# The second layer's experts as fp32 matmuls on two 64-column halves, with 22 weight tiles fetched ahead

## What is computed

```python
def _expert_choice_ffn(h, w_router, w_gate, w_up, w_down):
    b, t, d = h.shape                              # 1, 512, 1024
    cap = EC_CAPACITY_FACTOR * t // N_EXPERTS      # 64 rows for each of 16 experts
    aff = jax.nn.softmax(jnp.einsum('btd,de->bte', h, w_router).astype(jnp.float32), axis=-1)
    vals, idx = lax.top_k(aff.transpose(0, 2, 1), cap)
    xg = jax.vmap(lambda hb, ib: hb[ib])(h, idx)
    hid = jax.nn.silu(jnp.einsum('becd,edf->becf', xg, w_gate)) * jnp.einsum('becd,edf->becf', xg, w_up)
    out = jnp.einsum('becf,efd->becd', hid, w_down) * vals[..., None].astype(h.dtype)
    return jax.vmap(lambda ob, ib: jnp.zeros((t, d), h.dtype).at[ib.reshape(-1)].add(ob.reshape(-1, d)))(out, idx)
```

## Time and profile before

| | us |
|---|---|
| median of 3 runs | 4068.27 |
| lowest and highest | 4063.78, 4071.51 |
| span of the profiled execution (first to last instruction) | 4059.8 |
| the expert stage of the second layer in it: first router matmul | 1542.76 |
| first expert matmul | 1583.98 |
| last down matmul's end | 1882.94 |
| last sum of squares after the combination, its end | 1922.22 |

### The profile page before, as it was taken

The page is one execution under the profiler, slowest core; times in us unless marked ns, Lnnn a source line. Parts: engine busy times, 40 slices in busy tenths (PEclk is TensorE's granted clock), DMA queues, the critical chain, the costliest instruction groups (busy, mean ns, idle before and its releaser), DMA issues.

```text
span 4059.8 us, 52830 instructions
## 1 busy us (share of the span) xinstructions
...
## 2 busy tenths in 40 slices
PE   8998897998999587998999998899999999889998
...
GB/s 274 180 164 53 2 63 123 348 369 258 212 189 113 1 54 147 369 364 201 269 269 158 107 91 8 103 235 234 109 87 125 97 90 104 146 22 89 95 95 75
DMA packets 165090, 618.38 MB, mean 152 GB/s; under 512 B 18668, under 2 KB 20245, under 8 KB 163709
## 3 DMA queue, kind: packets, MB, share of 16 engines
...
...
## 4 chain that ended last, share of the span: by engine, by line
PE 83%; DVE 8%; ACT 4%; issue 2%; DMA 2%; SPq 0%; ACTq 0%; DVEq 0%; POOL 0%; POOLq 0%; PEldq 0%
PE psum L2243 23%; PE psum L2256 12%; PE psum L830 12%; PE psum L2011 8%; PE psum L915 5%; PE psum L2030 4%; PE psum L982 4%; PE psum L759 3%; PE psum L1199 1%; PE psum L1209 1%; PE psum L767 1%; DVE spare L1305 1%; DMA ring<-wtile 1%; PE psum L1967 1%; PE psum L1483 1%
## 5 line engine op out<-in xcount | busy, mean ns | idle before, releaser
L783 ACT CAST small_r<-ring 128x1024 fp32r<-128x1024 f32 x264 | 276.1, 1048 | 1075.1 <-PE psum L830 335.5
L787 DVE TENSOR_TENSOR ring_r<-ring,small_r 128x1024 fp32r<-128x1024 f32 x264 | 322.7, 1225 | 686.7 <-ACT small_r L783 686.2
L783 ACT CAST PB_r<-ring 128x1024 fp32r<-128x1024 f32 x344 | 357.5, 1050 | 567.8 <-PE psum L2243 326.8
L787 DVE TENSOR_TENSOR ring_r<-ring,PB_r 128x1024 fp32r<-128x1024 f32 x344 | 414.2, 1222 | 270.6 <-ACT PB_r L783 269.2
L2243 PE MATMUL psum<-H_r,ring_r 128*128 128x512 f32 x1344 | 335.2, 391 | 0.0
L2243 PE MATMUL psum<-H_r,small_r 128*128 128x512 f32 x1344 | 327.7, 396 | 0.0
L2243 PE MATMUL psum<-H_r,PB_r 128*128 128x512 f32 x1344 | 318.3, 389 | 0.0
L2243 PEld LDWEIGHTS psum<-H_r,small_r 128*128 128x128 f32 x1344 | 253.0, 188 | 60.8
L2243 PEld LDWEIGHTS psum<-H_r,ring_r 128*128 128x128 f32 x1344 | 252.2, 188 | 55.2
L2243 PEld LDWEIGHTS psum<-H_r,PB_r 128*128 128x128 f32 x1344 | 252.3, 188 | 53.2
L830 PE MATMUL psum<-H_r,small_r 128*128 128x512 f32 (+1 forms) x1040 | 275.0, 368 | 0.1
...
## 6 DMA issues: line engine op xcount, KB each, us to landing
ring<-wtile SPq DMA_DIRECT2D x800, 512.0 KB, 4.9
...
```

The costliest lines, as they stand in the source:

```text
L783: nc.scalar.copy(high(j), slot(g0 + j)).then_inc(high_ready.sem, 1)
L787: nc.vector.tensor_tensor(low(g0 + j), slot(g0 + j), high(j).bitcast(F32), ALU.subtract).then_inc(low_ready.sem, 1)
```

## The change

The routing moves word for word into a class `Routing`, which both layers use; layer 0 keeps `experts`. Layer 1 gets a function of its own, `latent_experts`:

- Weights and rows stay float32, nothing of them is split. In `gate_up` the gathered rows are loaded in both 64-column halves of the array; one half takes the first 256 hidden features, the other the last 256. A tile is 4 matmuls of 256 columns. In `down` each half takes 512 output features: a tile is 2 matmuls of 512 columns. Silu, product and the turn of the hidden rows are then 128 partitions high and 256 wide.
- Of the 192 tiles 22 leave the ring's stream, the second of each four up to tile 85 (`is_ahead`). They lie in an array of their own, `wahead`, and GpSimd fetches them to free parts of `PB` and `H`: 14 once all tiles ahead of the stage are used, 8 after the token rows are stored.
- The combination runs in four batches: pairs 0 to 3 in experts 9 to 12 (two feature tiles in each), pairs 4 and 5 in experts 13 and 14 (four in each), pair 6 in expert 15, pair 7 after the last down. Each batch is added to the residual by VectorE. The pairs' high parts have eight places, so no pair waits for another's.

```diff
+N_AHEAD = 22
+is_ahead = lambda i: i % 4 == 1 and i // 4 < N_AHEAD
...
-        plan += [(f"win_{l}", N_PT + 8), (f"wout_{l}", 8), (f"exp_{l}", 12 * N_EXP)]
+        plan += [(f"win_{l}", N_PT + 8), (f"wout_{l}", 8), (f"exp_{l}", 12 * N_EXP - l * N_AHEAD)]
...
+        def latent_experts(l, with_ctx, b_no):
...
+            M, PAIRS, HALF = CAP_LAT, N_EXP // 2, EXP_DIM // 2
+            routing = Routing(l, with_ctx, b_no)
...
+            places = tiles_at(PB, 8192, 6) + tiles_at(PB, 2048, 6) + tiles_at(PB, 20480, 2) + tiles_at(PB, 16384, 4) + tiles_at(H, 4096, 4)
+            bounds = [0, 3, 6, 10, 14, 18, N_AHEAD]
+            ring_no = lambda i: g0 + i - min(N_AHEAD, (i + 2) // 4)
+            used = lambda i: ring_no(i) + 1
+            in_tile = lambda e: 12 * e - 4 if e else 0
+            down_tile = lambda e: 12 * e + (16 if e < N_EXP - 1 else 8)
...
+            batches = [(0, 4), (4, 6), (6, 7), (7, 8)]
+            n_mix = KT * len(batches)
+            mixed_in = {9 + i: [(0, 2 * i), (0, 2 * i + 1)] for i in range(4)}
+            mixed_in |= {13 + i: [(1, 4 * i + k) for k in range(4)] for i in range(2)}
+            mixed_in[15] = [(2, k) for k in range(KT)]
+            last_bank = (5, 0, 1, 2, 3, 4, 6, 7)
+            mix_bank = lambda z, k: bank[last_bank[k] if z == len(batches) - 1 else (5, 1)[k % 2]]
...
+            def ten(eng):
+                routing.ten(eng)
+                def tile(i):
+                    if not is_ahead(i):
+                        filled(eng, ring_no(i))
+                        return slot(ring_no(i))
+                    if i // 4 in bounds:
+                        v = bounds.index(i // 4)
+                        eng.wait_ge(ahead_in[v].sem, 16 * (bounds[v + 1] - bounds[v]))
+                    return places[i // 4]
+                def rows_turn(e):
+                    eng.wait_ge(rows_in[e % 2].sem, b_in[e % 2] + 16 * (e // 2 + 1))
+                    for k in range(KT):
+                        mm = nc.tensor.transpose(bank[0][:, k * M:(k + 1) * M], XT[e % 2][:, k * P:(k + 1) * P], ident[0:M, 0:M])
+                    mm.then_inc(gath_ready.sem, 1)
+                def gate_up(e):
+                    eng.wait_ge(gath_copied.sem, b_gc + e + 1)
+                    for s in range(2):
+                        for q in range(4):
+                            i = in_tile(e) + 4 * s + q
+                            w = tile(i)
+                            for k in range(2):
+                                for o in range(2):
+                                    mm = nc.tensor.matmul(bank[2 + s][M * o:M * o + M, 0:HALF], XG[e % 2][:, 2 * q + k, :],
+                                                          w[:, EXP_DIM * k + HALF * o:EXP_DIM * k + HALF * (o + 1)], start=(q == 0 and k == 0), stop=(q == 3 and k == 1))
+                            if not is_ahead(i):
+                                mm.then_inc(tile_used, 1)
+                def hidden_turn(e):
+                    eng.wait_ge(hid_ready.sem, b_hi + e + 1)
+                    for c in range(2):
+                        mm = nc.tensor.transpose(bank[4][:, c * P:(c + 1) * P], hidden[:, c * P:(c + 1) * P], ident)
+                    mm.then_inc(hidT_ready.sem, 1)
+                def down(e):
+                    eng.wait_ge(hidT_copied.sem, b_hc + e + 1)
+                    if e >= 2:
+                        eng.wait_ge(down_copied.sem, b_dc + e - 1)
+                    for f in range(4):
+                        i = down_tile(e) + f
+                        w = tile(i)
+                        for s in range(2):
+                            mm = nc.tensor.matmul(bank[6 + e % 2][M * s:M * s + M, :], HIDT[:, f % 2, M * (f // 2):M * (f // 2) + M],
+                                                  w[:, 512 * s:512 * s + 512], start=(f == 0), stop=(f == 3))
+                        if not is_ahead(i):
+                            mm.then_inc(tile_used, 1)
+                def mix(z, k):
+                    n, (first, end) = KT * z + k, batches[z]
+                    if k == 0:
+                        eng.wait_ge(mix_low.sem, b_ml + end)
+                        eng.wait_ge(spread_ready.sem, b_sw + end)
+                    if z < len(batches) - 1 and n >= 2:
+                        eng.wait_ge(mix_added.sem, b_ma + n - 1)
+                    if z == len(batches) - 1 and k == 0:
+                        eng.wait_ge(mix_added.sem, b_ma + n)
+                    for g in range(first, end):
+                        nc.tensor.matmul(mix_bank(z, k), high[g][:, k * P:(k + 1) * P], SWL[:, g, :], start=(g == first), stop=False)
+                        mm = nc.tensor.matmul(mix_bank(z, k), OUTL_R[:, g, k * P:(k + 1) * P], SWL[:, g, :], start=False, stop=(g == end - 1))
+                    mm.then_inc(mix_summed.sem, 1)
+                rows_turn(0)
+                for e in range(N_EXP):
+                    gate_up(e)
+                    if e + 1 < N_EXP:
+                        rows_turn(e + 1)
+                    if e:
+                        down(e - 1)
+                    hidden_turn(e)
+                    for z, k in mixed_in.get(e, ()):
+                        mix(z, k)
+                down(N_EXP - 1)
+                for k in range(KT):
+                    mix(len(batches) - 1, k)
...
+            def sca(eng):
+                routing.sca(eng)
+                def take(e):
+                    eng.wait_ge(gath_ready.sem, b_ga + e + 1)
+                    nc.scalar.copy(XG[e % 2].rearrange("p k m -> p (k m)"), bank[0]).then_inc(gath_copied.sem, 1)
+                def put(e):
+                    eng.wait_ge(tile_used, used(down_tile(e) + 3))
+                    r = slice(M * (e % 2), M * (e % 2) + M)
+                    for s in range(2):
+                        at = slice(M * s, M * s + M)
+                        ins = nc.scalar.activation(OUTL[r, e // 2, 512 * s:512 * s + 512], bank[6 + e % 2][at, :], ACT.Copy, scale=gate_of[at, e:e + 1])
+                    ins.then_inc(down_copied.sem, 1)
+                    if e % 2:
+                        eng.wait_ge(down_copied.sem, b_dc + e + 1)
+                        nc.scalar.copy(high[e // 2], OUTL[:, e // 2, :]).then_inc(mix_high.sem, 1)
+                take(0)
+                for e in range(N_EXP):
+                    eng.wait_ge(tile_used, used(in_tile(e) + 3))
+                    nc.scalar.activation(gated, bank[2][:, 0:HALF], ACT.Silu).then_inc(gate_ready.sem, 1)
+                    if e + 1 < N_EXP:
+                        take(e + 1)
+                    if e:
+                        put(e - 1)
+                    eng.wait_ge(hidT_ready.sem, b_ht + e + 1)
+                    nc.scalar.copy(HIDT.rearrange("p c m -> p (c m)"), bank[4][:, 0:HALF]).then_inc(hidT_copied.sem, 1)
+                put(N_EXP - 1)
...
+                def spread(g):
+                    nc.vector.tensor_scalar(SWL[:, g, :], cn("iota", 0, NLAT), row_lat[:, g:g + 1], None, ALU.is_equal).then_inc(spread_ready.sem, 1)
+                def low(g):
+                    eng.wait_ge(mix_high.sem, b_mh + g + 1)
+                    nc.vector.tensor_tensor(OUTL_R[:, g, :], OUTL[:, g, :], high[g].bitcast(F32), ALU.subtract).then_inc(mix_low.sem, 1)
+                def add(z, k):
+                    eng.wait_ge(mix_summed.sem, b_ms + KT * z + k + 1)
+                    nc.vector.scalar_tensor_tensor(Xv[:, k, 0:NLAT], mix_bank(z, k), mcol(0, 40 + k), Xv[:, k, 0:NLAT], ALU.mult, ALU.add).then_inc(mix_added.sem, 1)
+                for e in range(N_EXP):
+                    eng.wait_ge(tile_used, used(in_tile(e) + 7))
+                    eng.wait_ge(gate_ready.sem, b_gt + e + 1)
+                    nc.vector.tensor_tensor(hidden, gated, bank[3][:, 0:HALF], ALU.mult).then_inc(hid_ready.sem, 1)
+                    if e < PAIRS:
+                        spread(e)
+                    if e and e % 2 == 0:
+                        low(e // 2 - 1)
+                    for z, k in mixed_in.get(e, ()):
+                        add(z, k)
+                low(PAIRS - 1)
+                for k in range(KT):
+                    add(len(batches) - 1, k)
+            def poo(eng):
+                def bring(v):
+                    for x in range(bounds[v], bounds[v + 1]):
+                        eng.dma_start(places[x], wahead[x]).then_inc(ahead_in[v].sem, 16)
+                eng.wait_ge(tile_used, g0)
+                for v in range(4):
+                    bring(v)
+                routing.store(eng)
+                routing.stored(eng)
+                bring(4)
+                bring(5)
+                eng.wait_ge(index_ready.sem, routing.b_ix + 1)
+                for e in range(N_EXP):
+                    if e >= 2:
+                        eng.wait_ge(gath_ready.sem, b_ga + e - 1)
+                    routing.gather(eng, e, XT[e % 2], rows_in[e % 2])
+            stage(flowing=True, tensor=ten, scalar=sca, vector=vec, gpsimd=poo)
...
```

(5 more changed lines are left out.)

230 lines of the change are left out of this document (137 added, 93 removed).

## The result

The changed kernel takes **3997.91 us** (median of 4 runs, 3994.57 to 4005.4), the kernel before 4069.89 (4063.78 to 4074.99): ratio 0.9833, 95% interval 0.9818 to 0.9848. The forecast was 4000, range 3984 to 4022. The profiled execution took 3998.63 us, 1.8 more than its span of 3996.8.

What follows compares the result with a forecast made beforehand. DMA transfers were to become the bound: 161 x 1.295 + 14 x 2.1 = 238 us from about 1590, the stage ending at 1850.9 instead of 1922.2. So 4059.8 - 71.3 + 3 + 8.5 = 4000 us, range 3984 to 4022.

Steps and rivals of the forecast that it cites:

- 0.87 us a tile: TensorE's gate, up and down matmuls: two column halves run in the time of one; without overlap 1.75 us.
- the four tiling changes an expert: Rival: switching the tiling mode drains TensorE, an estimated 0.8 us an expert, inside 2.4 us spare; no chance of its own.
- 1.295 us a tile on the DMA engines: Expert loop: transfer time of one 524,288-byte weight tile at 405 GB/s, 161 of them counted.
- 2.1 us a gather: Expert loop: DMA time for one gather of token rows, shortfall plus own bytes, 0.84 MB; 14 counted, 29.4 us.
- The DMA queue full from 1590: Loop's start: transfers run without pause from about 1589 to 1590, after half clock until about 1588.
- The combination hidden in experts 9 to 14: Combination matmuls, 3.7 us an expert, fit beside transfers: 15.2 us of TensorE in a 17.6 us period.
- Expert 15 paced by VectorE: Loop's end: eight groups of two combination matmuls each wait for VectorE's 0.75 us add, 8 x 0.75.
- The last down matmul: End of expert 15: TensorE's down projection, 3.5 us, ends at 1834.5.
- The tail, 16.4 us: From last down matmul to the stage's last sum: 4.3 + 2.2 + 6.9 + 3.0 us, ending at 1850.9.
- Prefetch: Ahead of the loop: GpSimd's 14 tiles are in by 1560; first gather about 1 us late (0 to 15).
- The rival of late gathers: GpSimd's queue moves 250 GB/s, first gather waits until 1595: up to 15 us more, 4015; 0.13 with the clock.
- The clock rival: TensorE waiting for tiles gets half clock in experts 9 to 15: 19 us more, 4019; 0.13 with the gathers.

Runs made afterwards that it cites:

- the kernel with two gathers: Changed kernel with only the first two of its 16 gathers, experts 2 to 15 reusing those rows: median 3977.5 us, ratio 0.9782.
- the kernels with 24 tiles: Changed kernel, 24 instead of 22 tiles fetched ahead, additions first: with last batches merged 3989.0 us; with 8 gathers of 128 rows instead 3986.6 us.

## Why the prediction came out

The mechanism is the one that was forecast. That the number was hit within 2.1 us is in part luck: 12 us that were put too dear stand against 13 that were left out, and the scatter between executions is larger than the miss.

- **The bound changes hands.** Right: TensorE idles 18 of 208 us, the DMA engines carry 409 GB/s wherever no gather runs, and taking the tiles ahead away brings back 24.7 us.
- **0.87 us a tile.** Right, on the strength of one row with N = 128; without the halves it is 1.72, as the upper bound said (1.75). An expert on TensorE was put at 11.5 us; the kernel with two gathers shows 11.65. So the four tiling changes an expert, a rival at an estimated 0.8 us, cost 0.1 to 0.2 together at most.
- **1.295 us a tile on the DMA engines.** 1.28. Loads beside a TensorE-bound stage ran at 405; here they run at 409 to 410.
- **2.1 us a gather.** Wrong: 1.37, which made 14 gathers 10.2 us too dear, the largest error of the sum. The step that failed is the reading of the earlier trace rows: the 4-us stretches of before held more loss than the gather's. The ring there was held back by TensorE too (363 GB/s in the mean over 246 us in which TensorE never paused, and 356 to 360 in the 4 us ahead of the stretch), and the shortfall in bytes was put down to the gather alone: 0.58 MB, where 0.30 is the gather's. A price for an operation wants a stretch in which nothing else limits; the two microseconds of the trace after give it.
- **The DMA queue full from 1590.** Too early by some 3 us of transfers: in this trace that is 1595.8, and until 1600 the engines carry 237 instead of 409 GB/s, until 1612 still 339, in part because the first tiles are used at half clock (0.50 until 1594).
- **The combination hidden in experts 9 to 14.** The sum, 15.2 against a period of 17.6, left a margin of 2.4 us. For experts 9 to 13 that held. In expert 14 VectorE's order and the half clock behind it made 8.1 us of a piece of 3.7, longer than the eight slots last, and the transfers ran dry. This cost about 5 us that the forecast did not have: it had counted each engine's work, and not the order of VectorE's.
- **Expert 15 paced by VectorE.** Right: its mix takes 6.0 us (1828.56 to 1834.58; 8 x 0.75 was put) with short waits for the additions, and down of 15 follows it.
- **The last down matmul** was put at 1834.5 - 1542.8 = 291.7 us of the stage, and came at 289.6. The parts: gathers -10.2, tiles 161 x 0.013 = -2.1, start +3, expert 14's stall +5. They give -4.3; 2.2 us I can't assign.
- **The tail, 16.4 us.** 19.1: the first addition 4.6 us after the last down matmul (4.3), GpSimd's first 2.2 after that (2.2), its five 7.1 (6.9), and then 5.3 instead of 3.0 for the sums, since TensorE had idled and got half clock (0.50 at 1852 to 1855): L674 takes 3.25 us for four, where it took 1.9 to 2.0. The 3 us charged for this in the next stage were thus partly due in this one.
- **Prefetch.** 14 tiles in by 1564.1, that is 1558.3 in the time of the kernel before (1560 was put); the first gather's rows 1.26 us later (1), but 3.4 in the second trace of the same kernel. The rival of late gathers did not come, though the kernels with 24 tiles (4.3 and 4.6 us later) show that it begins right behind 22.
- **Sum.** Predicted gain of the stage 71.3, measured 70.7. Too dear by 12.3 us (gathers, tiles), too cheap by 12.9 (start 3, expert 14 about 5, tail 2.7, and 2.2 unassigned): that they cancel is luck. The offset of the median to the span was put at 8.5 us; the changed kernel's median is 1.1 us over its profiled span, but that execution had its 5.8 us in the earlier stages. Both offsets are scatter between executions, and the 7.4 us between them made up for the 5.3 by which the span was missed (3991.5 in the forecast's sum, 3996.8 measured).
- **The clock rival** had 0.13 with the gathers: the loop's clock is 0.99 over 208 us, though TensorE idles for 9% of the time. It fell only where the mix stalled for 2.3 us, and at the tail.
- The Trainium skill ("DMA: Bandwidth & Descriptors", Specifications) puts the HBM limit of a core at about 358 GB/s. With this one core running the trace has 380 over 208 us and 409 within them, so the forecast was right to go by its rows.
